# A decoder block on eight cores: head weights spread inside stage 0, one gate pair ahead of the late values, and the merge's five weight places from its seventh block on

## The chip, the cores and the metric

One Trainium2 chip; the program runs on all 8 cores, each with its own share of the work and no exchange between them. The metric is the device time in microseconds of the slowest core, as a median over executions.

## The reference

One layer over x of 4 x 2048 x 2048 (batch, tokens, width), cut to what matters:

```
h = rmsnorm(x) * g1
q, k, v, q_i, k_i, w_i, u_b, v_b, g_a, g_b = split(h @ w_in)      # w_in 2048 x 10320
# A: 8 heads of 128; 16 index heads of 64 choose 256 keys for each token
score[t,s] = sum_h w_i[t,h] * relu(q_i[t,h] . k_i[s]) * const      # causal
out_a = softmax(q.k/sqrt(128) + T5 bias, over the 256 keys of the highest score) @ v
# B: chunked gMLP, chunks of 128 tokens, 8 groups
out_b = gelu(u_b) * (tril(w_spatial) @ rmsnorm(gelu(v_b)) + b)
merged = sigmoid(g_a) * (out_a @ w_proj_a) + sigmoid(g_b) * (out_b @ w_proj_b)
x = x + merged @ w_out
x = x + (silu(h2 @ w_gate) * (h2 @ w_up)) @ w_down                 # h2 = rmsnorm(x) * g2, width 5632
```

## The kernel before

A batch has two cores; each owns 8 of the 16 blocks of 128 tokens and computes keys and values of all 16. The instructions of each engine are written out by a small planner in program order. It keeps a clock of its own for each engine, advanced by a cost for each operation; every engine then runs its list in order and waits on semaphores. Products of weights are cut into **units**: 16 (or 8) matmuls of 128x512 or 128x256 into one PSUM bank, then a consumer on ScalarE (ACT) or VectorE (DVE). A unit is queued in steps of 4 matmuls.

**Stages.** Stage 0 (`D0`, to about 323 us of the profile) normalizes x (`x_norm`, with the gain tile `GB`; `x_tr` transposes), makes values and keys of the first half, the queries q, the head weights w_i (`wi_unit`, 8 short units), the index keys (`ki_unit`, 4 units) and the index queries (`qi_unit`, 16 units with ACT consumers). Then comes what the code calls w2: the head weights, 128 tokens x 16 heads, are split in three bf16 parts (`w3`), spread over the partitions by 24 matmuls against `sel` (line 778), multiplied and summed into `absw`, and ACT takes the sign (`sgnw`). Every index tile needs `absw` and `sgnw`. `c_m4` holds the masks for it; SBUF of `GB` is reused.

The attention stage (about 341 to 868 us) works tile by tile in the order 0, 1, 2, 3, 7, 6, 5, 4. Tile k has index scores X (lines 930 and 914), a bisection B of 16 rounds on DVE that finds the threshold of the 256 best keys (line 285), a transpose of the mask T (line 1011), and attention C (lines 1042, 1077, 1108). While B of one tile runs, X of the next and C of the one before are issued. Where the planner's clock has PE waiting, it puts in a step of the **fill queue** `DD`: 16 key units of the second half, 32 value units, and 56 gate units (7 of 8 column blocks `c2`, two gates, 4 units each; tanh on ACT, then a store to DRAM `Gscr` by the SyncE queue, SP). Up to mark `'k'` the queue may be used from the start; behind it the queue is held (`DD.hold`) until the bisection of tile 2 is through, because the late values lie where the accumulator of tile 2 lies. What is not used before tile 6's scores of the values is forced there; `drain` gives fill to PE while a bisection ends; the rest runs after the last tile.

Stage 3 (`D3`, from about 868 us) makes v_b and u_b, the spatial gate (`sgu_z`), then the **merge**: 18 blocks of weights in the order g7 a7 a0 h7 b7 b0 a1 b1 ... a6 b6 (g, h: the eighth column block of the gates; a, b: w_proj_a and w_proj_b of 256 columns, 32 matmuls each), in which the stored gates are loaded back (`gl_load`, 8 x 256 KB for each c2, SP), then w_out (8 blocks) and the FFN.

**The weight ring.** Weights are loaded on the GpSimd queue (POOL) with a cast, into five places of 8 KB; places 3 and 4 serve other purposes in the attention stage. A block's place comes from `WS.cycle` when the block is declared. `pump` issues loads strictly in order: each as soon as the last block in its place is used up, and none before the one ahead of it. Places 3 and 4 open after a7 (`open_ring`).

Before the change the cycle of three stands at place 1 when the merge begins, and the cycle of five starts at the fifth block:

```
block   g7 a7 a0 h7 b7 b0 a1 b1 a2 b2 a3 b3 a4 b4 ...
before   1  2  0  1  1  2  3  4  0  1  2  3  4  0
after    1  2  0  1  2  0  3  4  0  1  2  3  4  0
```

Of the kernel before, what the change touches and what calls it, by code (L numbers as in the profile page):

```python
# [7 lines left out]
F32 = mybir.dt.float32  # L8
BF16 = mybir.dt.bfloat16
AF = mybir.ActivationFunctionType  # L10
# [189 lines left out]
def build(ncores=8):  # L200
# [32 lines left out]
    with ExitStack() as es:  # L233
# [69 lines left out]
        def dma_pool(out, in_, reads=(), writes=(), append=False):  # L303
            return P.dma('pool', lambda e: e.dma_start(out=out, in_=in_), reads, writes, append)  # L304
# [412 lines left out]
        def wi_unit(tt):  # L717
            n = tt // 4

            def cons(pi):  # L720
                dve('copy', (PS[pi],), (B_wt,), out=wtok[:, tt, :], in_=psb[pi][:, 0:16])
            unit(D0, kib, lambda s_, c: hX[n][:, c, (tt % 4) * 128:(tt % 4 + 1) * 128], lambda s_, c: s_[:, c, 128:144], 16,
                 lambda pi: psb[pi][:, 0:16], (B_h[n],), cons, 0.12)
        D0.add(0.1, ki_dup)
        for tt in range(8):
            wi_unit(tt)
        for hx in (HO0, HO1, HT0, HT1):
            ki_unit(D0, kib, hx)

        def qi_unit(blk, b, cc, n):  # L730
            def cons(pi):
# [12 lines left out]

        DD = Dense()
        kb2 = [wblock(w_in, 1024 + 256 * b, 256) for b in range(4)]
        vb2 = [wblock(w_in, 2048 + 256 * b, 256) for b in range(4)]
        NG = 7
        gab = [(g, c2, wblock(w_in, (6224 if g == 0 else 8272) + 256 * c2, 256)) for c2 in range(NG) for g in range(2)]
# [5 lines left out]
        B_w2 = Buf(after=(B_gb,))  # L755
        B_m4 = Buf()
        sel = R(191.5, 2 * KB, BF16, "p (g h q) -> p g h q", g=8, h=8)
        w3 = [R(193.5 + 0.25 * i, 256) for i in range(3)]
        wr = R(194.25, 512, F32)
        m4p = R(194.75, 544)  # L760
        wsum = [R(195.5 + 2 * i, 2 * KB, F32) for i in range(2)]
        wt_ = wtok.rearrange("p t h -> p (t h)")
        dma_pool(m4p, c_m4, (), (B_m4, B_w2))
        dve('copy', (B_c, B_w2), (B_w2,), out=sel,
            in_=ident.rearrange("p (g q) -> p g q", g=8).unsqueeze(2).broadcast_to([128, 8, 8, 16]))
        dve('copy', (B_wt, B_w2), (B_w2,), out=w3[0], in_=wt_)
        dve('tt', (B_wt, B_w2), (B_w2,), out=wr, in0=wt_, in1=w3[0], op=ALU.subtract)
        dve('copy', (B_w2,), (B_w2,), out=w3[1], in_=wr)
        dve('tt', (B_w2,), (B_w2,), out=wr, in0=wr, in1=w3[1], op=ALU.subtract)
        dve('copy', (B_w2,), (B_w2,), out=w3[2], in_=wr)  # L770
        for half in range(2):
            pi = (5, 6)[half]

            def spread(e, half=half, pi=pi):
                ins = None
                for g in range(4):
                    for j in range(3):
                        ins = e.matmul(psb[pi][:, 128 * g:128 * g + 128],
                                       sel[:, 4 * half + g, :, :].rearrange("p h q -> p (h q)"), w3[j],
                                       start=(j == 0), stop=(j == 2))  # L780
                return ins
            P.op('pe', spread, (B_w2,), (PS[pi],), cost=0.8)
        for half in range(2):
            pi = (5, 6)[half]
            dve('tt', (PS[pi], B_w2), (B_w2,), out=wsum[half].rearrange("p (x h) -> p x h", h=16),
                in0=psb[pi].rearrange("p (x h) -> p x h", h=16),
                in1=m4p[:, 256:272].unsqueeze(1).broadcast_to([128, 32, 16]), op=ALU.mult)
            dve('red', (B_w2,), (B_sw,), out=absw[:, 4 * half:4 * half + 4, :, :].rearrange("p g t a -> p (g t a)"),
                in_=wsum[half].rearrange("p (x h a) -> p x a h", h=8, a=2), axis=AX.X, op=ALU.add)
        act(sgnw, absw, AF.Sign, (B_sw,), (B_sw,))  # L790
        dve('tt', (B_sw,), (B_sw,), out=absw, in0=absw, in1=sgnw, op=ALU.mult)
        dve('copy', (B_w2, B_wt), (B_wt,), out=mask4.rearrange("p g c -> p (g c)"), in_=m4p[:, 0:256])
        xdone = B_xb + B_xn
        B_kT[1] = Buf('kT1', after=xdone)
        B_V[1] = Buf('V1', after=xdone)

        def v1_ones():
            B_V[1].absorb((B_acc[2],))
            P.op('dve', lambda e: e.memset(V[:, 8:16, :, 128:130], 1.0), (), (B_V[1],))
        for b in range(4):  # L800
            for cc in range(2):
                for hx in (HO1, HT1):
                    k_unit(DD, kb2[b], b, cc, hx)
        DD.mark('k')
        DD.hold = 'k'
        DD.add(0, v1_ones)
# [7 lines left out]
        B_G = {}  # L814
        gst_n = [0]

        def gate_unit(g, c2, blk, cc, n):
            def cons(pi):
                if gst_n[0] == 0:
                    for i in range(4):  # L820
                        B_gst[i] = Buf('gst', after=(B_h[HT1],))
                i = gst_n[0] % 4
                gst_n[0] += 1
                act(GST[i], psb[pi], AF.Tanh, (PS[pi],), (B_gst[i],), scale=0.5)
                B_G[g, c2, cc, n] = Buf()
                dma_sp(Gscr[g, 2 * c2 + cc, n], GST[i], (B_gst[i],), (B_G[g, c2, cc, n],))
            fm_unit(DD, blk, cc, lambda c: hX[n][:, c, :], B_h[n], cons)
        for (g, c2, blk) in gab:
            for cc in range(2):
                for n in range(2):  # L830
# [854 lines left out]
```

How the kernel before makes its waits and increments, by code:

```python
            def run(name, e):  # L1557
                for waits, fn, inc in P.q[name]:
                    for k, v in waits:
                        e.wait_ge(sems[k], v)
                    if fn is None:
                        continue
                    ins = fn(e)
                    ins.then_inc(sems[inc[0]], inc[1])
```

## Time and profile before

| | us |
|---|---|
| median of 3 runs (2195.71 to 2333.64) | 2197.43 |
| the profiled execution's own time | 2204.41 |
| its span (core 3, the slowest) | 2202.8 |
| span of the other cores | 2178.3 to 2193.7 |
| PE busy (94% of the span) | 2069.9 |
| DVE / ACT / POOL busy | 754.0 / 581.4 / 233.9 |

The profile is of one execution, on its slowest core. PE is TensorE's matmul stream, and its idle time ahead of an operation is put down to what ended it. The granted clock is a share of full speed: 0.5 is 1.2 GHz, 1.0 is 2.4 GHz. Two of the three runs lie within 1.72 us of each other.

### The profile page before, as it was taken

To read this page: it belongs to the slowest core of one execution; us is meant where nothing else is said; L and a number is where in the kernel's file an instruction comes from. 1 tells how busy PE (TensorE), PEld (TensorE's weight loads), DVE (VectorE), ACT (ScalarE), POOL (GpSimd) and SP (SyncE) were. 2 spreads that over 40 slices of the span, in tenths; PEclk is the share of its full clock that TensorE was granted. 3 is DMA by queue.
4 is the path that set the end of the run, shared out by engine and by line. 5 is a ranking of instruction groups with operands and counts; after the bars stand their busy time and mean duration, and the time that the engine had idled before them with its cause. 6 is when DMAs were issued, how large, how long until landed. Compare 5 with 4: busy or idle time off the path is not lost.

```text
span 2202.8 us, 36223 instructions; the slowest of 8 cores (2178.3 to 2202.8 us)
## 1 busy us (share of the span) xinstructions
PE 2069.9 (94%) x13650; PEld 1223.6 (56%) x13650; DVE 754.0 (34%) x1450; ACT 581.4 (26%) x1012; POOL 233.9 (11%) x273
## 2 busy tenths in 40 slices
PE   3899988879999997997997999999999999999999
PEld 3754433348435465843456854444588744444888
DVE  2333206877867876132651431111111111111111
ACT  3455414666666653410000230000000000000000
POOL 1000010000000000101110011111111111111110
PEclk8999998979999998998998999999999999999999
DMA  9895452405564655546999165555566755555675
GB/s 209 188 167 93 72 76 41 58 20 83 102 113 102 111 111 131 78 58 124 230 204 150 21 77 77 77 77 77 65 80 73 91 77 77 77 77 65 107 112 120
DMA packets 313691, 217.50 MB, mean 99 GB/s; under 512 B 17328, under 2 KB 288048, under 8 KB 311216
## 3 DMA queue, kind: packets, MB, share of 16 engines
q0 software_dynamic: 272976, 137.22, 50.6%
q1 hardware_dynamic: 40544, 77.96, 11.1%
q8 instruction: 112, 1.84, 0.3%
q14 instruction: 59, 0.48, 0.1%
HBM read 326.14 MB, written 27.79 MB: 161 GB/s over the span
## 4 chain that ended last, share of the span: by engine, by line
PE 86%; DMA 5%; DVE 4%; ACT 2%; issue 2%; another core or an unknown queue 0%; DVEq 0%; POOL 0%; ACTq 0%; POOLq 0%; SPq 0%
PE ps L310 65%; PE ps L1506 14%; DVE arena L285 2%; ACT arena L265 2%; PE ps L930 2%; DMA arena<-w_out 2%; PE ps L1042 2%; PE ps L914 2%; PE ps L1077 1%; DMA arena<-w_in 1%; DVE arena L286 1%; DVE arena L284 1%; DMA arena<-w_pb 1%; PE ps L478 1%; PE ps L499 0%
## 5 line engine op out<-in xcount | busy, mean ns | idle before, releaser
L310 PE MATMUL ps<-arena 128*128 128x512 bf16 (+2 forms) x8384 | 1574.6, 346 | 51.0 <-DMA arena<-w_pb 15.6
L310 PEld LDWEIGHTS ps<-arena 128*128 128x128 bf16 x8384 | 807.6, 99 | 764.4 <-issue 92.3
L265 ACT ACTIVATE arena<-ps 128x512 f32<-128x512 f32 (+5 forms) x450 | 260.8, 582 | 1126.5 <-PE ps L310 982.1
L1506 PE MATMUL ps<-arena 128*128 128x256 bf16 x2816 | 307.9, 273 | 3.3 <-DVE arena L284 2.6
L1506 PEld LDWEIGHTS ps<-arena 128*128 128x128 bf16 x2816 | 275.3, 98 | 36.3 <-issue 4.5
L284 DVE TENSOR_TENSOR arena<-ps,arena 128x512 bf16<-128x512 f32 (+2 forms) x130 | 85.6, 658 | 586.5 <-PE ps L310 540.2
L265 ACT ACTIVATE arena<-ps,arena 128x512 bf16<-128x512 f32 (+1 forms) x388 | 223.4, 655 | 50.8 <-PE ps L930 38.6
L304 POOL DMA_DIRECT2D arena<-w_in x98 | 86.0, 887 | 882.7 <-PE ps L310 544.6
L285 DVE TENSOR_SCALAR_CACHE_REDUCE arena<-arena 128x512 bf16<-128x512 f32 (+6 forms) x112 | 172.6, 1541 | 5.6
L265 ACT ACTIVATE arena<-arena 128x2048 bf16<-128x2048 f32 (+4 forms) x135 | 97.2, 721 | 259.6 <-PE ps L310 220.3
L284 DVE TENSOR_TENSOR arena<-arena 128x512 bf16<-128x512 bf16 (+8 forms) x313 | 126.2, 430 | 70.1 <-ACT arena L265 30.0
L284 DVE TENSOR_TENSOR arena<-arena,ps 128x256 f32<-128x256 f32 x128 | 53.9, 421 | 256.7 <-PE ps L1506 256.7
L286 DVE SCALAR_TENSOR_TENSOR arena<-arena 128x1 f32<-128x1 f32 (+2 forms) x151 | 91.7, 611 | 109.6 <-ACT arena L265 85.8
L286 DVE SCALAR_TENSOR_TENSOR arena<-ps,arena 128x256 f32<-128x256 f32 (+1 forms) x116 | 66.0, 569 | 183.1 <-PE ps L310 93.1
L304 POOL DMA_DIRECT2D arena<-w_down x48 | 41.1, 860 | 301.3 <-PE ps L1506 227.1
L304 POOL DMA_DIRECT2D arena<-w_up x44 | 38.5, 880 | 291.1 <-PE ps L310 278.9
L286 DVE SCALAR_TENSOR_TENSOR arena<-arena,ps 128x512 f32<-128x512 f32 x64 | 44.0, 687 | 69.3 <-PE ps L310 60.8
L304 POOL DMA_DIRECT2D arena<-w_gate x44 | 38.5, 879 | 260.3 <-PE ps L310 252.4
L1077 PE MATMUL ps<-arena 128*128 128x129 bf16 x576 | 57.8, 226 | 4.9 <-DVE arena L284 2.9
L285 DVE TENSOR_SCALAR arena<-ps,arena 128x512 bf16<-128x512 f32 (+1 forms) x76 | 51.7, 697 | 29.9 <-PE ps L930 29.9
L930 PE MATMUL ps<-arena 64*128 64x512 bf16 (+1 forms) x304 | 46.9, 389 | 13.3 <-ACT arena L265 5.1
L1042 PE MATMUL ps<-arena 128*128 128x128 bf16 x576 | 56.9, 226 | 1.7 <-ACT arena L265 1.3
(43 smaller groups left out, 411.6 us busy)
## 6 DMA issues: line engine op xcount, KB each, us to landing
arena<-w_in POOLq DMA_DIRECT2D x96, 512.0 KB, 8.6
arena<-w_gate POOLq DMA_DIRECT2D x44, 512.0 KB, 7.8
arena<-w_up POOLq DMA_DIRECT2D x44, 512.0 KB, 7.4
arena<-x_perm SPq DMA_DIRECT2D x16, 1024.0 KB, 9.8
arena<-w_down POOLq DMA_DIRECT2D x32, 512.0 KB, 8.5
gscr<-arena SPq DMA_DIRECT2D x56, 256.0 KB, 2.7
arena<-gscr SPq DMA_DIRECT2D x56, 256.0 KB, 8.5
arena<-x_perm SPq DMA_DIRECT2D x32, 256.0 KB, 13.3
```

The lines of the kernel that those rows point to most:

```text
L265: return P.op('act', lambda e: e.activation(out=out, in_=in_, func=func, **kw), reads, writes, cost=0.2 + 0.9e-3 * n)
L284: 'tt': lambda e: e.tensor_tensor(**kw),
L285: 'ts': lambda e: e.tensor_scalar(**kw),
L286: 'stt': lambda e: e.scalar_tensor_tensor(**kw),
L304: return P.dma('pool', lambda e: e.dma_start(out=out, in_=in_), reads, writes, append)
L310: ins = e.matmul(out, pairs[i][0], pairs[i][1], start=(i == 0), stop=(i == n - 1))
L478: ins = e.transpose(pv[:, c * 128:(c + 1) * 128], xn_[:, cc * 128:(cc + 1) * 128], ident)
L914: ins = e.matmul(psb[G[4]][64 * t:64 * t + 64, 0:wc], Wg[:, u + 4 * t, a, :], pl[2 * t + a][0][:, 0:wc], start=(u == 0 and a == 0), stop=( ...
L930: ins = e.matmul(psb[G[2 * t + a]][:, 0:wc], qsrc[64 * a:64 * a + 64, (k % 4) * 8 + u + 4 * t, :, :].rearrange("p h q -> p (h q)"), kiT2[6 ...
L1042: ins = e.matmul(psb[pl][:, (j - g0) * 128:(j - g0 + 1) * 128], kblk(h, j), qT[:, h, kc], start=True, stop=True)
L1077: ins = e.matmul(psb[po][:, hh * 130:hh * 130 + 129], PT[pti][:, (j - g0) * 128:(j - g0 + 1) * 128], V[:, j, h, 0:129], start=(j == 0), st ...
L1506: ins = e.matmul(psb[tt][:, 0:256], aT[:, f0 + c, tt * 128:(tt + 1) * 128], slot[:, c, 0:256], start=(f0 + c == 0), stop=(f0 + c == 21))
```

## The change

Three edits, in the order of the program.

1. **Head weights in stage 0.** The load of `c_m4` moves from the POOL queue behind stage 0 to the SP queue ahead of the `wi_unit`s, as f32 with no cast, and `sel` is made there; the three-part split is placed behind the `wi_unit`s, and the 24 matmuls with their DVE and ACT work behind the `ki_unit`s, ahead of the `qi_unit`s. The two halves share one `wsum`.
2. **One gate pair early.** The 8 gate units of c2 = 0 (two weight blocks) are queued behind the late keys and ahead of mark `'k'`, so that they can be used before the values may. They use four own buffers (`GST0`, where late values will lie); `v1_ones`, a DVE memset ahead of the late values, now also waits for their stores.
3. **The ring.** The cycle of five starts at the seventh block of the merge. Of all blocks only b7 and b0 change their places (see the table above).

```diff
+        def w2_load():
+            B_w2.absorb((B_gb,))
+            dma_sp(m4p, c_m4, (), (B_m4, B_w2))
+            dve('copy', (B_c, B_w2), (B_w2,), out=sel, ...)
+        def w2_parts():
+            dve('copy', (B_wt, B_w2), (B_w2,), out=w3[0], in_=wt_)
+            ...                                  # 3 copies and 2 subtractions, moved
+        def w2_spread():
+            ...                                  # 24 matmuls, 2 x (multiply, reduce), Sign, multiply, copy, moved
         D0.add(0.1, ki_dup)
+        D0.add(0, w2_load)
         for tt in range(8):
             wi_unit(tt)
+        D0.add(0, w2_parts)
         for hx in (HO0, HO1, HT0, HT1):
             ki_unit(D0, kib, hx)
+        D0.add(0.8, w2_spread)
...
         kb2 = [wblock(w_in, 1024 + 256 * b, 256) for b in range(4)]
+        gab0 = gblocks(range(1))
         vb2 = [wblock(w_in, 2048 + 256 * b, 256) for b in range(4)]
-        gab = [... for c2 in range(NG) for g in range(2)]
+        gab = gblocks(range(1, NG))
         D0.run()
-        dma_pool(m4p, c_m4, (), (B_m4, B_w2))
-        ...                                      # all of w2 stood here
         def v1_ones():
-            B_V[1].absorb((B_acc[2],))
+            B_V[1].absorb((B_acc[2],) + tuple(B_gst0))
...
+        for (g, c2, blk) in gab0:
+            for cc in range(2):
+                for n in range(2):
+                    gate_unit(g, c2, blk, cc, n)
         DD.mark('k')
         DD.hold = 'k'
         DD.add(0, v1_ones)
...
-            if si == 4:
-                WS.cycle = [(j - (len(seq) - 4)) % 5 for j in range(5)]
+            if si == 6:
+                WS.cycle = [(j - (len(seq) - 6)) % 5 for j in range(5)]
```

## Rows read from the trace of the kernel before

**Rows 1.** The page, part 1: busy time, share of the span, instructions.

```profile
PE 2069.9 (94%) x13650; PEld 1223.6 (56%) x13650; DVE 754.0 (34%) x1450; ACT 581.4 (26%) x1012; POOL 233.9 (11%) x273
```

**Rows 2.** Waits of PE on core 3: us in total, times, longest.

```profile
PE ps L478 <- DVE arena L286: 25.0, 4, 15.2
PE ps L310 <- DMA arena<-w_pb: 15.6, 1, 15.6
PE ps L310 <- DMA arena<-w_out: 14.0, 3, 9.8
PE ps L778 <- DVE arena L287: 12.9, 1, 12.9
...
PE ps L1011 <- DVE arena L285: 9.4, 1, 9.4
```

**Rows 3.** The same view on core 7, the next slowest.

```profile
PE ps L310 <- DMA arena<-w_out: 7.1, 1, 7.1
```

**Rows 4.** Timeline, 323 to 347 us: start, length, engine, [idle before <- releaser].

```profile
323.12 0.60 ACT L265 ACTIVATE arena<-ps 128x512 bf16<-128x512 f32 x1 [2.86 <-PE ps L310]
325.24 0.57 POOL L304 DMA_DIRECT2D arena<-c_m  x1
333.49 0.43 DVE L287 COPY arena<-arena 128x1024 bf16<-128x1024 bf16 x1 [61.60 <-DMA arena<-c_m]
...
335.85 2.72 PE L778 MATMUL ps<-arena 128*128 128x128 bf16 x24 [12.88 <-DVE arena L287]
...
341.17 1.04 PE L930 MATMUL ps<-arena 64*128 64x512 bf16 x4 [2.61 <-DVE arena L284]
...
342.14 4.87 PE L310 MATMUL ps<-arena 128*128 128x512 bf16 x12
```

**Rows 5.** The chain that ended last: start, length, what.

```profile
957.59 3.45 PE ps L310 x16
```

**Rows 6.** Timelines of SP and DVE, 150 to 272 us.

```profile
180.18 30.55 SPq L301 DMA_DIRECT2D escr<-fscr  x48
...
223.98 2.35 DVE L286 SCALAR_TENSOR_TENSOR arena<-arena 128x2048 bf16<-128x2048 f32 x1 [0.95 <-ACT arena L265]
```

**Rows 7.** DMA issues: count, KB each, median us to landing.

```profile
arena<-c_cneg SPq DMA_DIRECT2D x1, 256.0 KB, 2.7
...
arena<-w_pb POOLq DMA_DIRECT2D x8, 512.0 KB, 22.5
```

**Rows 8.** Windows: length, busy PE PEld DVE ACT POOL, clock, DMA share, GB/s.

```profile
429.60:466.50 36.90, 21.79 (x136) 8.94 (x136) 27.70 (x76) 19.05 (x31) 1.77 (x2) 0.62 0.30 51
...
500.00:795.00 295.00, 293.87 (x2233) 157.79 (x2231) 214.99 (x435) 186.82 (x333) 24.61 (x28) 1.00 0.55 101
...
814.50:848.30 33.80, 24.41 (x117) 10.92 (x115) 28.38 (x60) 5.63 (x9) 3.50 (x4) 0.90 0.94 175
```

**Rows 9.** Timelines of PE and DVE, 810 to 850 us.

```profile
814.57 24.34 PE L310 MATMUL ps<-arena 128*128 128x512 bf16 x112
848.32 1.01 PE L1011 MATMUL ps<-arena 128*128 128x128 bf16 x8 [9.41 <-DVE arena L285]
...
810.26 1.54 DVE L285 TENSOR_SCALAR_CACHE_REDUCE arena<-arena 128x1280 bf16<-128x1280 f32 x1
...
847.29 0.89 DVE L285 TENSOR_SCALAR arena<-arena 128x1280 bf16<-128x1280 f32 x1
```

**Rows 10.** Timeline of POOL (weight loads) in the merge.

```profile
998.57 1.75 POOL L304 DMA_DIRECT2D arena<-w_in  x2 [14.06 <-PE ps L1294]
1027.11 1.75 POOL L304 DMA_DIRECT2D arena<-w_pb  x2 [26.79 <-PE ps L310]
...
1030.57 0.91 POOL L304 DMA_DIRECT2D arena<-w_pa  x1
...
1051.72 0.88 POOL L304 DMA_DIRECT2D arena<-w_pb  x1 [20.24 <-PE ps L310]
```

**Rows 11.** Windows in the merge, columns as in rows 8.

```profile
1010.00:1026.50 16.50, 16.50 (x77) 7.33 (x75) 1.52 (x3) 1.79 (x3) 0.00 (x0) 1.00 0.19 71
...
1042.00:1140.00 98.00, 97.88 (x445) 44.02 (x446) 58.45 (x85) 0.00 (x0) 14.86 (x17) 0.98 1.19 214
1140.00:1200.00 60.00, 46.05 (x381) 38.62 (x380) 11.93 (x27) 0.00 (x0) 5.25 (x6) 0.89 1.00 178
```

More of the change, by code:

```diff
@@ L723, in wi_unit @@
                  lambda pi: psb[pi][:, 0:16], (B_h[n],), cons, 0.12)
+        B_w2, B_m4 = Buf(), Buf()
+        sel = R(191.5, 2 * KB, BF16, "p (g h q) -> p g h q", g=8, h=8)
+        w3 = [R(193.5 + 0.25 * i, 256) for i in range(3)]
+        wr = R(194.25, 512, F32)
+        m4p = R(194.75, 1088, F32)
+        wsum = R(196, 2 * KB, F32)
+        wt_ = wtok.rearrange("p t h -> p (t h)")
+        def w2_load():
+            B_w2.absorb((B_gb,))
+            dma_sp(m4p, c_m4, (), (B_m4, B_w2))
+            dve('copy', (B_c, B_w2), (B_w2,), out=sel,
+                in_=ident.rearrange("p (g q) -> p g q", g=8).unsqueeze(2).broadcast_to([128, 8, 8, 16]))
@@ new lines, in w2_parts, with spread @@
+        def w2_parts():
+            dve('copy', (B_wt, B_w2), (B_w2,), out=w3[0], in_=wt_)
+            dve('tt', (B_wt, B_w2), (B_w2,), out=wr, in0=wt_, in1=w3[0], op=ALU.subtract)
+            dve('copy', (B_w2,), (B_w2,), out=w3[1], in_=wr)
+            dve('tt', (B_w2,), (B_w2,), out=wr, in0=wr, in1=w3[1], op=ALU.subtract)
+            dve('copy', (B_w2,), (B_w2,), out=w3[2], in_=wr)
+        def w2_spread():
+            for half in range(2):
+                pi = (5, 6)[half]
+                def spread(e, half=half, pi=pi):
+                    ins = None
+                    for g in range(4):
+                        for j in range(3):
+                            ins = e.matmul(psb[pi][:, 128 * g:128 * g + 128],
+                                           sel[:, 4 * half + g, :, :].rearrange("p h q -> p (h q)"), w3[j],
+                                           start=(j == 0), stop=(j == 2))
+                    return ins
+                P.op('pe', spread, (B_w2,), (PS[pi],), cost=0.8)
+            for half in range(2):
+                pi = (5, 6)[half]
+                dve('tt', (PS[pi], B_w2), (B_w2,), out=wsum.rearrange("p (x h) -> p x h", h=16),
+                    in0=psb[pi].rearrange("p (x h) -> p x h", h=16),
+                    in1=m4p[:, 256:272].unsqueeze(1).broadcast_to([128, 32, 16]), op=ALU.mult)
+                dve('red', (B_w2,), (B_sw,), out=absw[:, 4 * half:4 * half + 4, :, :].rearrange("p g t a -> p (g t a)"),
+                    in_=wsum.rearrange("p (x h a) -> p x a h", h=8, a=2), axis=AX.X, op=ALU.add)
+            act(sgnw, absw, AF.Sign, (B_sw,), (B_sw,))
+            dve('tt', (B_sw,), (B_sw,), out=absw, in0=absw, in1=sgnw, op=ALU.mult)
+            dve('copy', (B_w2, B_wt), (B_wt,), out=mask4.rearrange("p g c -> p (g c)"), in_=m4p[:, 0:256])
@@ L746, in build, with gblocks @@
         kb2 = [wblock(w_in, 1024 + 256 * b, 256) for b in range(4)]
+        NG = 7
+        def gblocks(c2s):
+            return [(g, c2, wblock(w_in, (6224 if g == 0 else 8272) + 256 * c2, 256)) for c2 in c2s for g in range(2)]
+        gab0 = gblocks(range(1))
         vb2 = [wblock(w_in, 2048 + 256 * b, 256) for b in range(4)]
-        NG = 7
-        gab = [(g, c2, wblock(w_in, (6224 if g == 0 else 8272) + 256 * c2, 256)) for c2 in range(NG) for g in range(2)]
+        gab = gblocks(range(1, NG))
         D0.run()
@@ L753, in build @@
             B_qT[k].w = list(B_qTn[k // 4].w)
[L755 to L762, printed above, removed]
-        dma_pool(m4p, c_m4, (), (B_m4, B_w2))
[L764 to L792, printed above, removed]
         xdone = B_xb + B_xn
@@ L803, in build, with gate_unit, cons @@
                     k_unit(DD, kb2[b], b, cc, hx)
+        GST0 = [R(80 + 2 * i, 2 * KB, F32) for i in range(4)]
+        B_gst0 = [Buf('gst0', after=xdone) for _ in range(4)]
+        B_G = {}
+        def gate_unit(g, c2, blk, cc, n):
+            def cons(pi):
+                if c2 == 0:
+                    t_, b_ = GST0, B_gst0
+                else:
+                    t_, b_ = GST, B_gst
+                    if B_gst[0] is None:
+                        for i in range(4):
+                            B_gst[i] = Buf('gst', after=(B_h[HT1],))
+                i = gst_n[0] % 4
+                gst_n[0] += 1
+                act(t_[i], psb[pi], AF.Tanh, (PS[pi],), (b_[i],), scale=0.5)
+                B_G[g, c2, cc, n] = Buf()
+                dma_sp(Gscr[g, 2 * c2 + cc, n], t_[i], (b_[i],), (B_G[g, c2, cc, n],))
+            fm_unit(DD, blk, cc, lambda c: hX[n][:, c, :], B_h[n], cons)
+        gst_n = [0]
+        for (g, c2, blk) in gab0:
+            for cc in range(2):
+                for n in range(2):
+                    gate_unit(g, c2, blk, cc, n)
         DD.mark('k')
@@ L813, in build @@
         B_gst = [None] * 4
[L814 to L827, printed above, removed]
         for (g, c2, blk) in gab:
```

## The prediction

> **What bounds the kernel now.** I read four views. The page's first part says TensorE (PE) is busy 94% of the span [rows 1]: 2202.8 - 2069.9 = 132.9 us of idle time, plus what PE loses at half clock, is all that an edit which adds and removes no product can win. PE's waits name the large pieces of it [rows 2]; the reader is to see that three of the first five are touched here: line 778 (edit 1), w_pb (edit 3), and line 1011 (edit 2, as will be seen). The timeline tells what each wait hangs on, and the windows tell which engine sets the length of a stretch. A full-clock matmul of 512 columns costs 3.45 / 16 = 0.216 us [rows 5].
>
> **Edit 1, the head weights.** Before, the last index-query unit ends where its ACT copy starts, at about 323.0. The load of c_m4 is issued at 325.24, behind the weight loads in POOL's queue, and DVE gets to work at 333.49; the 24 matmuls start 12.88 us after PE fell idle, tile 1's scores 2.61 us after those [rows 4]. So 323.0 to 341.17, 18.2 us, holds 2.72 us of work. After it, the first 4 matmuls of line 930 and 12 of fill run at half clock: 12 x 0.216 = 2.6 us of fill took 4.87 [rows 4].
> What the change removes from the path: 18.2 us, less what the scores still wait for (the last ACT copy, 323.12 + 0.60, about 0.9 us after 323.0), gives 17.3. The 24 matmuls come back inside stage 0 at full clock, half of 2.72, 1.4. The slow restart goes: 4.87 - 2.6 = 2.3, and 0.5 of the 1.04 at line 930. Sum 17.3 - 1.4 + 2.8 = **18.7 us**. Bounds: if the clock isn't kept, 16; if the wait for the ACT copy vanishes too, 20.
> What it adds, queue by queue. SP: the new load waits for the last reader of GB, DVE's 2048-wide operation at 223.98 + 2.35 = 226.3; the SP queue is empty from 180.18 + 30.55 = 210.7 on, and a plain load twice its size landed in 2.7 us [rows 6, 7]. It lands near 229, and the `sel` copy that waits for it comes at about 245, so nothing is held. Were it late, the eight w_i copies would stand behind that copy on DVE, and PE behind its banks. DVE: the copy (0.43), five small operations and four of about 0.7 us are in stretches where DVE waits (its idle time up to 333.49 was 61.6 us [rows 4]). ACT: Sign waits some 3 us for the two sums, and ahead of the index-query copies; these come every 3.45 us, with five banks, so PE doesn't feel it. POOL loses one issue. One `wsum` in place of two costs nothing, since DVE is in order anyway. I price all of this at 0, at most 2 us if DVE's or ACT's order catches a bank.
>
> **Edit 2, the gate pair.** 8 units x 16 x 0.216 = 27.6 us of matmuls, in 32 steps, move to the front of the held queue. The key fill ends at 429.6, and from there to 466.5 PE has only scores and attention of small tiles: 36.9 us at a clock of 0.62 [rows 8]. At full clock that work is 12.1 us (14 groups of four 512-wide at 0.55, and about 80 of 128 columns at 0.055). DVE is busy 27.7 of the 36.9 us, and alternates with PE and ACT, so the length is theirs. Spare room on PE: 36.9 - 12.1 = 24.8 us, or 28 to 29 steps. So nearly the whole pair is swallowed, at -1 (the scores come back faster at full clock) to +3 us.
> What does that buy? The fill left at 466.5 is 32 value and 56 gate units, 353 steps with the memset. From 814.57 to 838.9 the last 28 of them (112 matmuls, 24.34 us) run in the last drain, then PE waits 9.41 us for tile 4's bisection, which DVE does from 810.26 to 848.2 without a break [rows 9]. The planner inserts fill where its own clock sees PE waiting, so the stretch between asks for the same 325 steps as before; after the change 353 - 28 = 325 are left for it, and the drain finds the queue empty. Its length is DVE's and stays. In other words the idle time moves: from the hold (36.9 - 21.8 = 15 us idle, and 21.8 - 12.1 = 10 us of half clock) to the drain (9.4 to some 34 us). Only steps beyond 28 come out of the stretch from 500 to 795, where PE is busy 293.87 of 295 us and fill really costs time [rows 8]: at most 4 x 0.86 = 3.5 us won, and the same paid in the hold. What is new is the memset's wait: it now waits for the last gate stores (a tanh, 0.6, and a store, about 2.7), and behind it on DVE stand tile 7's first relus and on ACT the value copies, which free PE's two fill banks. No row shows this; between 0 (all gates done earlier) and 4 us (gate unit directly ahead). Eight tanh of 0.6 us replace idle ACT time (19.05 of 36.9 us busy). The net of edit 2 is between +5 us and -5 us; I take **0**, since both ends of the move are stretches of DVE's length.
>
> **Edit 3, the ring.** b7 shares place 1 with h7, which runs directly ahead of it, so its load is issued at 1027.11, when h7 ends, and PE waits 15.6 us [rows 2, 10]; b0, a1, b1 and a2 stand behind it in order. After, b7 takes a7's place: issued near 1004, needed near 1027. b0 follows at a0's end, 1011, with a1 and b1. The DMA share is only 0.19 (71 GB/s) from 1010 to 1026.5 [rows 11], so 2 MB of loads have room there, and the wait goes: **15.6 us**.
> The price: a2 had been issued at 1030.57, four blocks early; now it waits for b0 in place 0 and is issued with b2 and a3 at b0's end, two blocks (2 x 32 x 0.216 = 13.8 us) before its use. A w_pb load took 22.5 us at the median, but with the gate loads in flight [rows 7]; the one at 1027.11 was there in 14.9 us beside x and gate loads. At b0's end the queues should have been emptied, as one load has the queue to itself first, so a2 is just in time: 0 to 5 us of new wait.
> From 1042 to 1140 the DMA share is 1.19, and PE still doesn't wait; from 1140 on it waits 14.0 us for w_out here, 7.1 on core 7 [rows 2, 3, 11]. With everything 15.6 us closer to the idle stretch, what counts is how much DMA work moves in there: 16.5 us x (1 - 0.19) = 13.4 us of room. So of 15.6 us, 13.4 are sure even if the rest is bound by transfers, less what a2 costs. I take **14**, bounds 5 and 15.6.
> Beside this the Trainium skill, page "DMA: Bandwidth & Descriptors", section "Issuing engines are not separate DMA queues", states that transfers started from different engines run on the same 16 DMA engines and interleave, so a change of order gives no bandwidth. The share of 1.19 agrees. By that rule alone the merge's end would be set by bytes and the wait would come back at w_out; that is the first rival.
>
> **The sum.** 18.7 + 0 + 14 = 32.7 us. The profiled execution: 2204.41 - 32.7 = 2171.7. It lies 7.0 us over the median, and its core 3 waits 6.9 us more for w_out than core 7 [rows 2, 3], so the median run stands for a core with less of that wait. On the median: 2197.43 - 32.7 = 2164.7; I say **2165**.
>
> **The rivals.**
> A: *Transfers bound the merge.* The wait at b7 goes, and comes back at a2 or w_out. For: share 1.19 from 1042 on, and 14.0 us of waits behind it. Against: 13.4 us of free DMA time ahead. It leaves 0 to 5 us of edit 3: 2197.4 - 18.7 - 3 = 2176.
> B: *The pair wins time.* The planner puts all 32 steps in the hold without lengthening it, the middle loses 4 steps and the chain of tiles 3 and 7 runs faster at full clock: 5 to 10 us more, 2157. For: a clock of 0.62 in the hold. Against: DVE's 27.7 us.
> C: *The pair costs time*: memset wait 4 us and a hold longer by 4: 2173.
> D: *Slower than before.* The gate steps lengthen the hold by their full 27.6 us, as each stands between a score and its relu, and with the queue dry before the drain PE idles through tile 5's end at 1.2 GHz, where some 13 us of attention matmuls cost double. With the memset's 4 us: 27.6 + 13 + 4 = 44.6 against 32.7 gained: 2209. It decides once edit 2 costs over 33 us. Against: 24.8 us of room in the hold.
> E: *Edit 1 doesn't do what it says*: c_m4 lands late on the SP queue, DVE stands at `sel`, and PE waits at the w_i units nearly as long as it did before, so that 3 us of edit 1 are left: 2197.4 - 14 - 3 = 2180. Against: 16 us of margin.
>
> **Chances.** Forecast (2160 to 2170) 0.45, A 0.22, B 0.15, C 0.12, D 0.03, E 0.03. The range leaves out D and the far ends of A and B: 2152 to 2181. A measurement of this kernel can tell about 2% from no change, 44 us: faster by over 2% is below 2153.5, the far end of B (edits 1 and 3 at their best, 20 + 15.6, and 8 more): 0.08. Slower by over 2% is above 2241: 0.01. Within 2%: 0.91.
>
> **What would show it.** Right: no c_m wait and no idle time over 2 us at line 778; scores of tile 1 some 17 to 18 us earlier; a clock near 1.0 in the hold and about 27 us of 512-wide fill in it; no fill in the last drain, and a wait of 30 us or more at line 1011; no w_pb wait at b7. Wrong: the last drain still has fill (the middle asked for less); the 300 us behind the hold shorter or longer by more than 5 us; a w_pa or w_pb wait at a2, or w_out waits that sum to over 20 us.

## The result, and the profile after

The changed kernel took 2169.95 us (median of 5 runs, lowest 2163.47). The kernel before, run beside it, took 2202.45 (5 runs). The ratio is 0.9853, with a 95% interval of 0.9829 to 0.9876: 32.5 us less, where 32.7 were forecast. That is less than the 2% which can be told from no change by the bound that the chances used, so the case falls in "within 2%". The forecast of 2165 stood on a median before of 2197.43; of the 5 us between 2165 and 2169.95, nearly all is that the kernel before itself came out 5.0 us higher this time. Some executions, of this kernel as of the one before, run slower at a lower granted clock (2443.43 us is one of the five), and every ratio here is taken without them.

The profiled execution took 2163.47 us. Core 5 is the slowest, with a span of 2161.9; the other cores lie between 2152.0 and 2161.9. [Rows 1] are answered by the window over the whole span (columns as in rows 8), which has all 13,650 matmuls:

```profile
0.00:2162.00 2162.00, 2050.90 (x13650) 1215.87 (x13650) 754.40 (x1450) 580.69 (x1012) 233.25 (x272) 0.98 0.66 101
```

Idle time of PE is 2161.9 - 2050.9 = 111.0 us, against 132.9 before. So of the 40.9 us between the two spans 21.9 us were idle time. The other 19.0 are busy time, though no product went; I put them down to the granted clock, a mean of 0.982 on this core against 0.971 before. PE's waits on core 5, which answer to [rows 2]:

```profile
PE ps L1034 <- DVE arena L285: 34.5, 1, 34.5
PE ps L478 <- DVE arena L286: 24.8, 5, 14.4
...
PE ps L310 <- DMA arena<-w_pb: 4.2, 1, 4.2
...
PE ps L310 <- DMA arena<-w_out: 1.1, 1, 1.1
```

Lines have moved by 23: 1034 is 1011 before, 953 is 930, 1131 is 1108. The wait of 12.9 us at line 778 is gone, w_pb went from 15.6 to 4.2, w_out from 14.0 to 1.1, and the wait for tile 4's bisection grew from 9.4 to 34.5. The cores differ (core 5 here, core 3 before), so what each edit is worth is read further down from means over the cores.

**Edit 1.** The timeline of SP and PE, where [rows 4] stood:

```profile
225.38 0.34 SPq L301 DMA_DIRECT2D arena<-c_m  x1
...
266.34 1.50 PE L754 MATMUL ps<-arena 128*128 128x128 bf16 x24
...
323.25 0.61 PE L953 MATMUL ps<-arena 64*128 64x512 bf16 x4
323.79 2.76 PE L310 MATMUL ps<-arena 128*128 128x512 bf16 x12
```

The load goes out at 225.38, the 24 matmuls run at full clock in 1.50 us without a wait, and tile 1's scores begin at 323.25, not 341.17. The 12 matmuls of fill behind them take 2.76 us where they took 4.87.

**Edit 2.** The windows of the hold and of the last drain (columns as in rows 8), which answer to [rows 8]:

```profile
409.00:444.00 35.00, 33.80 (x225) 15.70 (x226) 27.43 (x76) 22.17 (x36) 3.51 (x4) 1.00 0.65 107
444.00:462.00 18.00, 15.51 (x99) 8.20 (x97) 8.18 (x18) 9.14 (x17) 1.75 (x2) 0.91 0.77 117
...
801.00:836.00 35.00, 0.51 (x8) 0.36 (x8) 29.63 (x62) 1.02 (x1) 0.00 (x0) 0.53 0.30 53
```

The hold has a clock of 1.00 where it had 0.62, and PE is busy 33.80 of 35 us where it was busy 21.79 of 36.9. The drain has no fill: 0.51 us of PE work in 35. The timeline of PE says the same beside [rows 9]:

```profile
800.91 0.61 PE L1131 MATMUL ps<-arena 128*128 128x128 bf16 x8 [2.27 <-DVE arena L284]
836.01 1.01 PE L1034 MATMUL ps<-arena 128*128 128x128 bf16 x8 [34.49 <-DVE arena L285]
```

The idle time moved from the hold to the drain, as forecast. What was put at 0 to 4 us, the memset's wait for the gate stores, is here at 457 us. Timeline of DVE, ACT and PE:

```profile
454.58 1.48 PE L310 MATMUL ps<-arena 128*128 128x256 bf16 x12
...
457.77 0.17 DVE L812 MEMSET arena<- 128x128 bf16 x1 [8.11 <-DMA gscr<-arena]
...
458.03 0.39 ACT L265 ACTIVATE arena<-ps 128x256 bf16<-128x256 f32 x1 [5.57 <-DVE arena L812]
...
458.56 3.80 PE L310 MATMUL ps<-arena 128*128 128x256 bf16 x20 [2.50 <-ACT arena L265]
```

DVE stands 8.11 us at the memset until the last gate store has landed. Behind the memset stand the value copies on ACT (5.57 us), and behind these PE, whose banks are full: it waits 2.50 us, and runs the next 20 matmuls of 256 columns in 3.80 us, where at full clock they cost 20 x 0.108 = 2.2. The granted clock of that stretch is 0.61:

```profile
458.50:462.40 3.90, 3.84 (x22) 2.69 (x24) 3.23 (x9) 2.83 (x6) 0.00 (x0) 0.61 1.19 136
```

The wait at the memset is 6.9 to 8.1 us on the eight cores, 7.5 in the mean.

**Edit 3.** Timeline of POOL in the merge, which answers to [rows 10]:

```profile
998.79 0.87 POOL L304 DMA_DIRECT2D arena<-w_pb  x1 [5.85 <-PE ps L310]
999.66 0.88 POOL L304 DMA_DIRECT2D arena<-w_pa  x1
1000.52 0.89 POOL L304 DMA_DIRECT2D arena<-w_pb  x1
1026.61 0.88 POOL L304 DMA_DIRECT2D arena<-w_pa  x1 [25.19 <-PE ps L310]
1027.47 0.89 POOL L304 DMA_DIRECT2D arena<-w_pb  x1
1028.33 0.90 POOL L304 DMA_DIRECT2D arena<-w_pa  x1
```

and of PE:

```profile
989.44 57.14 PE L310 MATMUL ps<-arena 128*128 128x512 bf16 x264
1050.80 106.55 PE L310 MATMUL ps<-arena 128*128 128x512 bf16 x672 [4.22 <-DMA arena<-w_pb]
```

b0, a1 and b1 now go out at 998.79 to 1000.52, into the stretch that had been nearly idle for the DMA engines. Block b7 is not waited for. But a2, b2 and a3 go out together at b0's end, and b2, issued at 1027.47, is what PE waits for until 1050.80: it landed some 23 us after its issue. Other cores wait at other blocks of the same kind. On core 3 the first wait is at a2, one block (32 matmuls) earlier, and further ones are at a4 and b4:

```profile
986.31 50.24 PE L310 MATMUL ps<-arena 128*128 128x512 bf16 x232
1038.17 27.79 PE L310 MATMUL ps<-arena 128*128 128x512 bf16 x128 [1.63 <-DMA arena<-w_pa]
```

**Where the time came from, by stretch.** The mean over the 8 cores of one profiled execution, since single cores differ (below). Scores: the start of the first row of line 930 (953). Tile ends: the rows of 8 matmuls at line 1108 (1131), the last product of each tile's attention; the tiles end in the order 0, 1, 2, 3, 7, 6, 5, 4. "Tail" is from the last of these to the end of the span.

| kernel | first scores | to end of tile 0 | tile 0 to 1 | tile 1 to 2 | tile 2 to 7 | tile 0 to tile 4 | tail | mean span |
|---|---|---|---|---|---|---|---|---|
| before | 339.6 | 29.4 | 78.9 | 74.5 | 175.0 | 496.8 | 1322.6 | 2188.4 |
| after | 322.0 | 27.4 | 82.3 | 78.2 | 172.8 | 501.5 | 1307.4 | 2158.3 |

So: 17.6 + 2.0 us won before tile 0 ends, 4.7 lost in the attention, 15.2 won in the tail, 30.1 in all.

### The profile page after: what moved, and what is told of

Read it like the earlier page. It is cut to its first block, busy times and chain, and to the rows that moved or that the text cites. A ratio compares the mean times of both kernels' runs of the same rounds, so it can differ in the third digit from the quotient of the medians.

```text
span 2161.9 us, 36063 instructions; the slowest of 8 cores (2152.0 to 2161.9 us)
## 1 busy us (share of the span) xinstructions
PE 2040.8 (94%) x13499; PEld 1214.5 (56%) x13650; DVE 753.9 (35%) x1450; ACT 580.2 (27%) x1012; POOL 233.6 (11%) x272
## 4 chain that ended last, share of the span: by engine, by line
PE 86%; DMA 6%; DVE 4%; issue 2%; ACT 2%; DVEq 0%; POOL 0%; ACTq 0%; SPq 0%; POOLq 0%
PE ps L310 64%; PE ps L1529 14%; DMA arena<-w_out 2%; DVE arena L285 2%; ACT arena L265 2%; PE ps L953 2%; DMA arena<-w_in 2%; PE ps L937 2%; DMA arena<-w_pb 1%; PE ps L1065 1%; PE ps L1100 1%; DVE arena L286 1%; PE ps L478 1%; DVE arena L284 1%; PE ps L499 0%
## 5 line engine op out<-in xcount | busy, mean ns | idle before, releaser
L310 PE MATMUL ps<-arena 128*128 128x512 bf16 (+2 forms) x8240 | 1554.4, 345 | 42.5 <-DVE arena L287 10.7
L310 PEld LDWEIGHTS ps<-arena 128*128 128x128 bf16 x8384 | 803.2, 98 | 742.1 <-issue 76.5
L265 ACT ACTIVATE arena<-arena 128x2048 bf16<-128x2048 f32 (+3 forms) x135 | 97.3, 721 | 214.8 <-PE ps L310 191.7
L1065 PE MATMUL ps<-arena 128*128 128x128 bf16 x576 | 55.5, 223 | 1.0 <-ACT arena L265 0.5
L478 PE MATMUL ps<-arena 128*128 128x128 bf16 x384 | 28.4, 233 | 26.0 <-DVE arena L286 26.0
```

Source lines behind the costliest of these rows:

```text
L265: return P.op('act', lambda e: e.activation(out=out, in_=in_, func=func, **kw), reads, writes, cost=0.2 + 0.9e-3 * n)
L310: ins = e.matmul(out, pairs[i][0], pairs[i][1], start=(i == 0), stop=(i == n - 1))
L478: ins = e.transpose(pv[:, c * 128:(c + 1) * 128], xn_[:, cc * 128:(cc + 1) * 128], ident)
L1065: ins = e.matmul(psb[pl][:, (j - g0) * 128:(j - g0 + 1) * 128], kblk(h, j), qT[:, h, kc], start=True, stop=True)
```

## The experiments

The three edits were first made one at a time, then parts of them. A diff below is cut to its main lines (`...`) and is taken against the changed kernel, but for the load alone, which is taken against the kernel before.

**Edit 1 alone.** The new w2 functions in stage 0, with the pair and the cycle as before:

```diff
-        gab0 = gblocks(range(1))
-        gab = gblocks(range(1, NG))
+        gab = gblocks(range(NG))
...
-            if si == 6:
-                WS.cycle = [(j - (len(seq) - 6)) % 5 for j in range(5)]
+            if si == 4:
+                WS.cycle = [(j - (len(seq) - 4)) % 5 for j in range(5)]
```

> Edit 1 alone on the kernel before. If the sum of the prediction is right, it wins 18.7 us (ratio about 0.9915), or 20.7 us going by the trace of the changed kernel, where tile 1's queries end 20.7 us earlier; the wait for w_pb at b7 stays at 12 to 19 us, and the last drain keeps its 24 us of fill and its wait of 9.4 us at the mask transpose. The rival, that the 18 to 20 us are partly given back later because every weight load is asked for earlier, expects 12 us or less (ratio 0.9945 or more).

Measured: 2178.71 us, ratio 0.9886 (0.9849 to 0.9922). The stretches are read from a second run of the same kernel:

> Edit 1 alone once more, for its trace. Theory: first scores at 322 to 324 us on all cores, 78 to 79 us between the ends of attention of tiles 0 and 1 as before, the wait at b7 still 12 to 19 us; 19 to 20 us better than before core by core. Rival: the weight loads, asked for 20 us earlier, lose part of it on the way to the merge, so that the end of the last tile is less than 17 us earlier.

Measured: 2187.32, ratio 0.992 (0.9902 to 0.9937). The stretches: scores at 323.9, 27.4 to tile 0's end, 496.9 for the attention, tail 1324.6. So 15.7 + 2.0 us are won ahead of tile 0's end and the attention is as before. The tail is 2.0 us longer, within what it differs by among the kernels that have it unchanged (1320.3 to 1327.2); it has the w_pb wait as it was and a w_out wait much as before (core 7, waits of PE):

```profile
PE ps L310 <- DMA arena<-w_pb: 15.9, 1, 15.9
PE ps L310 <- DMA arena<-w_out: 12.6, 3, 7.1
```

The forecast of 18.7 us would be a ratio of 0.9915, which lies in both intervals. The two measurements give 25 and 18 us, so the metric alone does not fix the size; the stretches do.

**Edit 2 alone.** The w2 block and the cycle as before, the pair early.

> Edit 2 alone on the kernel before. Theory: the pair only moves idle time from the hold to the last drain and adds a wait of the memset for the gate stores, so it costs 5 to 9 us (ratio 1.002 to 1.004), a wait of about 34 us stands at the mask transpose of the last tile, and the memset waits for a gate store on DVE. Rival: the pair costs nothing by itself (within 2 us), and the 8 us that the changed kernel lost between tile 1 and tile 3 come from its meeting edit 1. A third, that it wins by the higher clock in the hold: ratio 0.998 or less.

Measured: 2202.78, ratio 1.0006 (0.9982 to 1.0029). Stretches: 82.6 and 76.4 for tiles 0 to 1 and 1 to 2, 172.8 for 2 to 7, 500.3 for the attention against 496.8. The memset waits here too (timeline of DVE, core 0):

```profile
473.75 0.17 DVE L803 MEMSET arena<- 128x128 bf16 x1 [5.85 <-DMA gscr<-arena]
```

In the stretches the pair costs 3.5 us, less than the 5 to 9 that were expected; the timed ratio can't tell that from 0. The memset waits 5.8 us in the mean here and 7.5 in the changed kernel, and the stretch from tile 1 to tile 2 is longer there by the same 1.7 us (78.2 against 76.5): what the pair costs more beside edit 1 is a longer wait for the store.

**Edit 3 alone.** The w2 block and the gates as before, the cycle from the seventh block on.

> Edit 3 alone on the kernel before. Theory: the wait of 12 to 19 us at b7 goes, 3 to 7 us of it come back as a wait for w_pb or w_pa at a2 or b2, whose loads are issued together when b0 ends, and waits for w_out get shorter or stay: 10 to 15 us won (ratio 0.993 to 0.9955). Rival, transfers bound the merge: the waits for w_pa, w_pb and w_out together shrink by 5 us or less (ratio 0.998 or more).

Measured: 2186.72, ratio 0.9924 (0.9892 to 0.9956), 16.7 us. Tail 1309.9, 12.7 us shorter; everything ahead of it as before (attention 496.7). On its slowest core, 6, the wait at line 778 stands, and part of the w_out wait:

```profile
PE ps L778 <- DVE arena L287: 15.1, 1, 15.1
...
PE ps L310 <- DMA arena<-w_out: 7.6, 3, 4.5
```

**Edits 1 and 3, without the pair.**

```diff
-        gab0 = gblocks(range(1))
-        gab = gblocks(range(1, NG))
+        gab = gblocks(range(NG))
...
-            B_V[1].absorb((B_acc[2],) + tuple(B_gst0))
+            B_V[1].absorb((B_acc[2],))
```

> Edits 1 and 3 without the early gate pair. Theory (the pair costs 6 to 8 us): 36 to 40 us won against the kernel before (ratio 0.982 to 0.984), 6 to 8 us better than the changed kernel, no wait of the memset, and 24 us of fill back in the last drain. Rival (the pair is harmless or helps): the same as the changed kernel, ratio 0.985 or more.

Measured: 2169.01, ratio 0.9849 (0.9816 to 0.9882). With the pair it is 0.9853 (0.9829 to 0.9876), so the pair is worth nothing that the metric shows; the 6 to 8 us that were expected from leaving it out did not come. Stretches: 322.6, 27.4, 78.5, 74.4, 175.0, attention 497.0, tail 1308.9. The attention is as long as before, so what it loses in the changed kernel (4.5 us against this one) comes with the pair.

**The load alone.** The kernel before, with only the load of `c_m4` on the SP queue ahead of the w_i units, as f32; `sel`, the split and the 24 matmuls stay behind stage 0. (The two halves share one `wsum`, as in edit 1.)

```diff
+        def w2_load():
+            B_w2.absorb((B_gb,))
+            dma_sp(m4p, c_m4, (), (B_m4, B_w2))
         D0.add(0.1, ki_dup)
+        D0.add(0, w2_load)
...
-        dma_pool(m4p, c_m4, (), (B_m4, B_w2))
```

> The kernel before with only the load of c_m4 moved to the SP queue ahead of the w_i units, as f32; the spreading of the head weights stays behind stage 0. Theory by the rows: PE no longer waits for the transfer, but for the sel copy and five small operations of DVE (333.49 to 335.8 us, 2.4 us), the 24 matmuls at 1.5 to 2.7 us and the 2.6 us to the first scores: of 18.2 us between stage 0 and the first scores 7 to 8.5 are left, 10 to 11 us won, half of edit 1 (ratio 0.995). Rival: the c_m4 transfer is not what DVE waits for, but a place in its queue, and nothing is won.

Measured: 2185.3, ratio 0.9939 (0.99 to 0.9977). First scores at 326.0 on six cores (on cores 2 and 3 PE ran slower in stage 0, they come at 352, and are left out). So the load alone gives 13.6 of the 17.6 us, or about 14: the kernels that leave stage 0 alone have their first scores at 339.6, 340.2 and 341.0. Timeline of PE, core 0:

```profile
320.56 1.50 PE L781 MATMUL ps<-arena 128*128 128x128 bf16 x24
...
324.67 0.61 PE L933 MATMUL ps<-arena 64*128 64x512 bf16 x4 [2.61 <-DVE arena L284]
```

With the load out of the way, DVE makes `sel` and the three parts from 269.56 to 271.8 on this core, while stage 0 still runs, since nothing but the load held them; the 24 matmuls then go in at full clock. What is left for the move of the matmuls is 4 us: themselves, 1.50, and the wait of 2.61 for the two sums. More came from the load alone than either theory had allowed, because both put `sel` and the split behind stage 0 as they stand in the program.

**The pair ahead of the last key block.** Gate units run before the last 4 key units, so that their stores have time to land. (The loop over the key blocks ahead is cut to three.)

```diff
-        kb2 = [wblock(w_in, 1024 + 256 * b, 256) for b in range(4)]
+        kb2 = [wblock(w_in, 1024 + 256 * b, 256) for b in range(3)]
         gab0 = gblocks(range(1))
+        kb2.append(wblock(w_in, 1024 + 256 * 3, 256))
...
+        for cc in range(2):
+            for hx in (HO1, HT1):
+                k_unit(DD, kb2[3], 3, cc, hx)
         DD.mark('k')
```

> The changed kernel with the early gate pair queued ahead of the last key block, not behind it, so that the gate stores have long landed when the memset of the value ones comes. Theory: of the pair's cost (between the end of attention of tile 0 and that of tile 2: 160.5 us in the mean of the cores with the pair, 153 without), some 4 us are the memset's wait for the gate stores and the slow restart behind it: that stretch falls to 156 to 157 us, and PE shows no wait for ACT at the first value units. The time is 2 to 4 us under the changed kernel's. Rival: the wait is covered, and the stretch is long because the hold is overfull: 160 us as before. In both cases the last drain stays empty of fill, with a wait of 34 us at the mask transpose.

Measured: 2175.84, ratio 0.9887 (0.9871 to 0.9902). My theory was that the memset's wait is most of what the pair costs, and that without it 2 to 4 us come back. The memset no longer waits, and yet the stretch from tile 1 to tile 2 grew from 78.2 to 81.6 us, that from tile 2 to 7 from 172.8 to 176.3, and the attention to 507.6. Timeline of DVE and PE, core 5:

```profile
438.65 1.16 PE L310 MATMUL ps<-arena 128*128 128x512 bf16 x4 [2.43 <-DVE arena L286]
...
454.40 0.17 DVE L813 MEMSET arena<- 128x128 bf16 x1
454.79 0.60 PE L310 MATMUL ps<-arena 128*128 128x256 bf16 x4 [2.41 <-DVE arena L813]
...
461.08 0.60 PE L310 MATMUL ps<-arena 128*128 128x256 bf16 x4 [2.97 <-DVE arena L286]
```

and the groups of instructions of the table loads, on core 4, with those of the changed kernel (core 5) below them:

```profile
L265 ACT ACT_TABLE_LOAD x9 | 11.5, 1283 | 10.8 <-DMA arena<-x_perm 7.2 <-PE ps L310 3.2 <-issue 0.2
```

```profile
L265 ACT ACT_TABLE_LOAD x7 | 9.0, 1283 | 8.3 <-DMA arena<-x_perm 7.0 <-PE ps L310 1.0
```

A key unit is not done with its product: it is normalized (a reduction, ln and exp on ACT, a multiply on DVE), and PE's banks wait for that chain. Last in the hold, these chains take the place of the store's wait (the three waits of PE above are 7.8 us). The 3.5 us from tile 2 to 7 are fill: 72 value matmuls of 256 columns run there in place of 40, and 32 x 0.108 is 3.5. Each change between the gates' tanh and the keys' ln and exp also loads ACT's tables again, 1.283 us, two more in all than in the changed kernel; on core 5 one of them lies in the hold, at 434.55, so they are a small part. The Trainium skill, page "ScalarE: Activation LUTs", section "What ACT_TABLE_LOAD costs", gives about 1283 ns for the load, and the trace agrees. In the same section the Trainium skill adds about 1380 ns of drain for every switch. Here the measurement differs: on core 5 of this run ACT's last operation ends 0.02 us ahead of the load, and the next one starts 0.02 us behind it (timeline of ACT).

```profile
432.69 1.84 ACT L265 ACTIVATE arena<-ps,arena 128x512 bf16<-128x512 f32 x3
434.55 1.28 ACT L265 ACT_TABLE_LOAD   x1
435.85 0.60 ACT L265 ACTIVATE arena<-ps 128x512 f32<-128x512 f32 x1
```

The theory, as a way to win, has fallen. What the memset's wait costs was left to the next experiment.

**Half the pair.** Only the first gate's 4 units (one weight block) of c2 = 0 are early.

```diff
-        gab0 = gblocks(range(1))
-        gab = gblocks(range(1, NG))
+        gab0 = [(0, 0, wblock(w_in, 6224, 256))]
+        gab = [(1, 0, wblock(w_in, 8272, 256))] + gblocks(range(1, NG))
...
-                if c2 == 0:
+                if c2 == 0 and g == 0:
```

> The changed kernel with one gate of the pair (4 units, 16 steps, 13.8 us) ahead of mark k, the other behind the late values. Theory: 13.8 us fit into the hold without filling it, and the stores have landed when the memset comes, so of the pair's cost nothing is left: the stretch from the end of attention of tile 0 to that of tile 2 is 153 to 155 us (160.5 with the pair, 153 without), and half of the fill is back in the last drain (wait at the mask transpose some 21 us in place of 34). 3 to 5 us better than the changed kernel core by core. Rival: any gate unit ahead of the memset puts its store in front of it, and the stretch is 157 us or more.

The changed kernel was run once more beside it:

> The changed kernel once more, for the comparison with the half pair on one chip. Theory: ratio 0.985 as measured first, so that the pair's 4 us (0.2%) lie within the interval; the half pair is ahead by 3 to 5 us. Rival: no order between the two, since waits for w_out of 0 to 13 us on one core or another set the slowest core.

Measured: half the pair 2175.7, ratio 0.9861 (0.9839 to 0.9883); the changed kernel 2174.12, ratio 0.9862 (0.9843 to 0.9882). Not to be told apart on the metric. The traces can tell: 81.6 and 75.7 us for tiles 0 to 1 and 1 to 2, against 82.3 and 78.5; the attention takes 498.4 against 501.7. The sum of the two stretches, 157.3, is what the rival expected (157 or more), though its reason, a store ahead of the memset, is not there: the memset waits for nothing (timeline of DVE, core 4).

```profile
441.96 0.17 DVE L812 MEMSET arena<- 128x128 bf16 x1
```

and the last drain's wait is between the other two kernels' (core 4, waits of PE):

```profile
PE ps L1034 <- DVE arena L285: 26.6, 1, 26.6
```

Windows of core 4 (columns as in rows 8) say where the time goes. The first line of each kernel runs from the last product of tile 0's attention to that of tile 1, the second from there to that of tile 2. Edits 1 and 3 without the pair:

```profile
351.24:429.67 78.43, 65.38 (x382) 26.01 (x387) 64.87 (x171) 47.99 (x83) 5.26 (x6) 0.94 0.50 60
429.67:504.04 74.37, 66.70 (x558) 41.90 (x560) 55.41 (x141) 52.87 (x99) 3.49 (x4) 0.87 0.28 33
```

Half the pair:

```profile
351.34:432.97 81.63, 75.52 (x444) 30.86 (x452) 68.27 (x180) 52.56 (x90) 5.41 (x7) 1.00 0.49 61
432.97:508.71 75.74, 70.44 (x622) 47.45 (x623) 52.03 (x132) 53.01 (x101) 5.09 (x6) 0.95 0.44 57
```

The changed kernel, with the whole pair:

```profile
349.95:432.19 82.24, 78.42 (x462) 31.63 (x461) 68.97 (x180) 52.51 (x90) 6.08 (x7) 1.00 0.46 58
432.19:510.06 77.87, 75.40 (x635) 47.26 (x634) 51.12 (x132) 54.19 (x103) 6.16 (x8) 1.00 0.56 84
```

From tile 0 to tile 1 DVE's idle time is the same in all three (13.6, 13.4, 13.3 us). What is longer is DVE's own work: nine more of its instructions, 3.4 to 4.1 us, stand ahead of tile 1's last product, with half the pair as with the whole, and the next stretch has nine fewer. So these 3 to 4 us are not lost there; the end of tile 1 has moved behind work that was to be done anyway. The loss is from tile 1 to tile 2, where DVE's idle time goes from 19.0 us to 23.7 with half the pair and 26.8 with the whole.

With the whole pair that is the memset's wait, 7.2 us on this core. On the 24 cores of the three traces that have the whole pair, the stretch from tile 1 to tile 2 grows with the wait about one for one: 76.5 us at a mean wait of 5.8, 78.2 at 7.5, 78.5 at 7.7. With half the pair the wait is gone but only about 3 us come back, since DVE now waits 12.0 us for scores from PE between tiles 1 and 2 (mean of the cores), against 8.3 with the whole pair and 5.1 without.

**Other places in the ring.** Edits 1 and 3 without the pair, with the first cycle of five turned so that a2 takes h7's place, which is free two blocks earlier than b0's.

```diff
             if si == 6:
-                WS.cycle = [(j - (len(seq) - 6)) % 5 for j in range(5)]
+                WS.cycle = [3, 4, 1, 2, 0]
...
-        WS.cycle = [0, 1, 2]
+        WS.cycle = [1, 2, 0]
         ob += [wblock(w_out, 256 * b, 256) for b in range(5, 8)]
```

> Edits 1 and 3 without the pair, and another order of the five places from the seventh block on: 3, 4, 1, 2, 0 in place of 3, 4, 0, 1, 2, so that a2 takes h7's place, b2 that of b7 and a3 that of b0, and their loads are issued one by one from h7's end on, not together at b0's end. Theory: the waits of 1.5 to 7 us for w_pa and w_pb (5 us in the mean of the cores) come from the late issue and go, to under 1.5 us in the mean; the waits for w_out stay between 0 and 13 us, core by core. 3 to 5 us better than without this (ratio to before about 0.983). Rival: transfers are the bound, and what is won at w_pa and w_pb comes back at w_out, so that the sum of the three in the mean of the cores stays at 7 to 8 us.

Measured: 2167.72, ratio 0.9845 (0.9825 to 0.9864). POOL's timeline on core 3 shows that a2 goes out at 1009.98, not with b2 and a3 at b0's end:

```profile
997.70 0.89 POOL L304 DMA_DIRECT2D arena<-w_pb  x1
1009.98 0.88 POOL L304 DMA_DIRECT2D arena<-w_pa  x1 [11.38 <-PE ps L310]
1016.70 0.87 POOL L304 DMA_DIRECT2D arena<-w_pb  x1 [5.84 <-PE ps L310]
```

and yet PE's waits for w_pa, w_pb and w_out, as a mean of the cores, are 6.6 + 2.0 = 8.6 us, against 5.1 + 3.2 = 8.3 without the turn. The turn does what it was made for: without it six of the eight cores wait at a2 or b2, with it none does. But the waits now stand at a3 to b5, and the 3 to 5 us that were expected did not come: another order of the places moves the waits and takes nothing away from them.

**Half the gate loads.** Edits 1 and 3 without the pair; of the 48 loads of 256 KB that bring the stored gates back in the merge, the 24 of the second gate are left out. The merge then works with gate values that aren't those of its block; all its instructions on PE, DVE and ACT stay.

```diff
-            for g in range(2):
+            for g in range(1):
```

> Edits 1 and 3 without the pair, with the stored second gate not loaded back in the merge (24 of 48 loads of 256 KB left out; the merge multiplies what lies in the buffer). Theory: the waits for w_out are a matter of bytes and go to under 1 us on every core; those for w_pa and w_pb behind b0 shrink to under 2 us, since the three loads issued together no longer share the DMA engines. Rival: w_out is late because its loads are issued late (a place is free only when a block of the merge ends), and waits of several us stay on some cores.

Measured, one run: 2152.17 us, cores 2144.0 to 2150.6. Windows of 120 us in the merge, first of the kernel with all loads (core 5), then of this one (core 7):

```profile
985.00:1105.00 120.00, 117.69 (x541) 52.75 (x539) 61.92 (x91) 2.39 (x4) 19.23 (x22) 0.99 1.16 217
```

```profile
985.00:1105.00 120.00, 117.36 (x539) 52.79 (x538) 61.92 (x90) 2.39 (x4) 18.36 (x22) 0.99 1.05 173
```

With 217 GB/s brought down to 173, no core waits for w_pa, w_pb or w_out at all, and the mean tail falls from 1308.9 to 1300.5, by the 8.3 us of waits that were there. So what the ring leaves over is the transfers' doing, not the places'. Leaving loads out takes away their number as well as their bytes, and this run can't part the two; the DMA share falls only from 1.16 to 1.05.

## Why the prediction was right

The sum was 18.7 + 0 + 14 = 32.7 us and 32.5 came. That closeness is luck: the interval of the ratio allows 27 to 38 us, the stretches add up to 30.1, and the same kernel run again took 2174.12, where 2169.95 had been just inside the forecast's 2160 to 2170. The terms were not all as right as the sum.

**Edit 1, 18.7 us.** Shown: 17.6 us at the first scores and 2.0 us of restart, 19.6 in all; 17.7 in the second run of edit 1 alone (15.7 and 2.0). Both its pieces, the wait and the half clock behind it, are in the rows, and the bounds of 16 and 20 held. No cost appeared on SP, DVE or ACT, and rival E is out: the load lands well before its use. What was misjudged is unspoken, that all of w2 has to move: the load alone was worth 13.6.

**Edit 2, 0 us.** The mechanism held in each piece: nearly the whole pair goes into the hold, the middle asks for less fill, 175.0 down to 172.8 us from tile 2 to 7 and 0.8 us more from tile 6 to 5, where 3.5 had been the most, and the idle time turns up in the last drain. The term is mis-sized. It costs 3.5 to 4.9 us in the stretches (500.3, 501.5 and 501.7 against 496.8), inside the bounds of -5 and +5 but at their end. Against the kernel without the pair, 7.6 us are lost between the ends of tiles 0 and 2, and 3.1 come back behind them. What was mis-sized is the memset's wait, put at "between 0 and 4" and then netted away. It is 7.5 us, and between 5.8 and 7.7 us the stretch grows with it one for one. Taking it away together with half of the fill gives back only about 3 us, and here "spare room on PE: 24.8 us" was too simple: in a hold in which PE is busy 33.80 of 35 us a score can stand behind steps of fill that it did not stand behind before, and DVE waits longer for it. Why that wait is longest with half the pair no run shows. Rival C had the mechanism (4 us for the memset, 4 for the hold); its net of 8 is the loss up to tile 2, without what comes back. Rivals B and D are out. On the metric the pair is not seen: 0.9853 and 0.9862 with it, 0.9849 without.

**Edit 3, 14 us.** The tail is shorter by 12.7 us in edit 3 alone, and over all traces it is 1310.4 us as the mean of the seven traces that have the edit and all loads (1307.4 to 1312.2), against 1323.7 as the mean of the four that don't have the edit (1320.3 to 1327.2): 13.3 us. The timed ratio of the edit alone gives 16.7. The wait at b7 is gone in all of them. The 0 to 5 us that were put against it for a2 are there: w_pa and w_pb waits of 5.0 us as a mean of the cores against 16.0 before, though spread over a2 to a5 and b2 to b5, and not at a2 alone. So one of the signs of being wrong, a w_pa or w_pb wait at a2, did appear, within the 0 to 5 us allowed for it. The gain agrees with the reason given, 13.4 us of free DMA time at the merge's start, but no run varied that free time. For what is left, the mechanism of rival A is borne out: one other order of the places did not take it away, and fewer loads did. Rival A's price, that the wait comes back nearly whole, does not hold.

**The profile against the median.** The two profiled executions differ by 40.9 us, the medians by 32.5, the means over cores by 30.1. The prediction saw one reason, that core 3 waits longer for w_out than core 7. It looks like the main one: as the mean of the cores, the w_out wait is 3.9 us before and 0.6 in the profiled run after; but core 6 of the repeated run of the same kernel has 14.9 us of it, and is its slowest with a span of 2182.8.

## What to carry to other kernels

Price a fill's move by the engine that sets each stretch, and compare that engine's idle time, not the length of the stretch alone, since a boundary can move. A hold in which PE is 40% idle could be filled here, but the new buffers put a store's landing in front of an engine that runs in order, and within what was measured each microsecond of that wait lengthened the stretch by one. Of a block of work that waits behind a late load, try the load alone first; here it was 13.6 of 17.6 us. When the order of weight loads is mended, ask how much free DMA time lies ahead, and test with loads taken away whether the rest is a matter of order at all.

## What the runs showed that I had not expected

The wait for w_out differs from core to core and from run to run of one program: 0 to 15 us, with the same instructions on each core. As the time is that of the slowest core, this alone moves single executions by some 10 us, and a gain of a few microseconds on each core can't be seen behind it.

A key unit behind a gate unit costs ACT a table load of 1.283 us each way, so the order of the fill decides not only what PE runs but how many of these there are (9 against 7).

A DVE memset of 0.17 us waits 7.5 us for a store to land, and holds copies on ACT and value matmuls on PE behind it.
